# An encoder step on one core: the first norm by tiles, queries ahead of keys, the first values as parts, fp32 averages, and two output tiles on GpSimd

## The reference, cut to what matters

```python
def rms_norm(x, g):
    y = x * lax.rsqrt(jnp.mean(x * x, axis=-1, keepdims=True) + EPS)
    return y * g
for l in range(DEPTH):
    h = rms_norm(xp, ln_mix[l])
    qa, ka, va, fa, qb, kb, vb = split(h @ w_in[l])
    logf = log_sigmoid(fa + b_f)
    c = cumsum(logf)                       # decay of each key, per head
    # 8 forgetting heads of 64, causal, softmax(q k * scale + c_q - c_k) @ v
    # then: sliding-window heads, output projection, memory attention, gated convolution
y = rms_norm(x, ln_final)
```

## Time and profile before

| what | value |
|---|---|
| median of 3 runs | 3360.53 us (3358.93 to 3365.29) |
| the profiled execution's own time | 3357.14 us |
| its span, first to last instruction | 3355.3 us |
| granted TensorE clock, mean | 0.991 |
| busy: TensorE 96%, weight loads 93% | VectorE 56%, POOL 36%, ScalarE 25% |
| moved by DMA | 177.57 MB |

### The profile page before, as it was taken

One profiled execution on the slowest core, in us unless ns is written; L12 is line 12 of the kernel. 1 busy time (PEld: TensorE's weight loads), 2 busy tenths in 40 slices (PEclk: granted clock), 3 DMA queues, 4 the chain that ended last, 5 costly groups with the idle time before them and its releaser, 6 DMA issues.

```text
span 3355.3 us, 50277 instructions
## 1 busy us (share of the span) xinstructions
PE 3219.7 (96%) x20496; PEld 3110.7 (93%) x20496; DVE 1893.9 (56%) x3526; ACT 843.9 (25%) x1950; POOL 1210.8 (36%) x976
## 2 busy tenths in 40 slices
PE   7999998999999999999999999989999999999997
PEld 7888898888999999999988988978889999999996
DVE  6655557676744444444665656576756444444445
ACT  4432324543300000000233333154433000000002
POOL 5213223542433333333442122443425333333331
PEclk9999999999999999999999999999999999999998
DMA  4111222211111111111122111321111111111111
GB/s 161 52 52 45 65 66 69 64 45 31 37 44 46 45 45 46 43 45 47 39 78 59 52 52 46 92 68 51 42 29 42 45 45 45 42 45 47 45 45 65
DMA packets 86021, 177.57 MB, mean 53 GB/s; under 512 B 10544, under 2 KB 13872, under 8 KB 85392
## 3 DMA queue, kind: packets, MB, share of 16 engines
q1 hardware_dynamic: 71968, 132.90, 13.7%
q10 hardware_dynamic: 13824, 41.46, 4.3%
HBM read 150.36 MB, written 16.29 MB: 50 GB/s over the span
## 4 chain that ended last, share of the span: by engine, by line
PE 80%; DVE 10%; ACT 6%; issue 2%; POOL 1%; DMA 0%; ACTq 0%; DVEq 0%; SPq 0%; POOLq 0%
PE PS L614 80%; DVE ACC L1636 2%; ACT PR L1262 2%; DVE HL L1628 1%; DVE PR L1717 1%; DVE XT L1760 1%; ACT PW L1262 1%; DVE PW L1717 1%; ACT PTH L1114 1%; DVE XT L1590 1%; DVE PTL L1562 1%; POOL WL L594 1%; POOL WH L592 1%; DVE DG L1675 0%; ACT G0H L1114 0%
## 5 line engine op out<-in xcount | busy, mean ns | idle before, releaser
L592 POOL TENSOR_TENSOR WH<-RAW,zero 128x512 fp32r<-128x512 f32 x484 | 549.4, 1135 | 2059.1 <-PE PS L614 2044.5
L614 PE MATMUL PS<-HH,WH 128*128 128x384 f32 (+1 forms) x3312 | 861.6, 332 | 26.5 <-DVE HL L1628 17.1
L614 PE MATMUL PS<-HH,WL 128*128 128x384 f32 (+1 forms) x3312 | 848.9, 328 | 0.0
L614 PE MATMUL PS<-HL,WH 128*128 128x384 f32 (+1 forms) x3312 | 848.4, 328 | 0.0
L594 POOL TENSOR_TENSOR WL<-RAW,WH 128x512 fp32r<-128x512 f32 x484 | 666.8, 1378 | 37.9
L614 PEld LDWEIGHTS PS<-HH,WH 128*128 128x128 f32 x3312 | 587.1, 189 | 37.3 <-issue 19.3
L614 PEld LDWEIGHTS PS<-HL,WH 128*128 128x128 f32 x3312 | 590.2, 189 | 0.0
L614 PEld LDWEIGHTS PS<-HH,WL 128*128 128x128 f32 x3312 | 589.7, 188 | 0.0
L1760 DVE TENSOR_TENSOR XT<-PS,XT 128x320 f32<-128x320 f32 x464 | 314.3, 719 | 264.1 <-PE PS L614 264.0
L614 PE MATMUL PS<-G0H,WH 128*128 128x384 f32 (+1 forms) x960 | 274.9, 339 | 25.1 <-DVE XT L1590 16.4
L1114 ACT ACTIVATE PTH<-PS 128x512 fp32r<-128x512 f32 (+4 forms) x320 | 165.5, 520 | 493.7 <-PE PS L614 492.4
(11 more groups left out here) (255 smaller groups left out, 4704.4 us busy)
## 6 DMA issues: line engine op xcount, KB each, us to landing
RAW<-in_slabs SPq DMA_DIRECT2D x484, 256.0 KB, 2.6
XR<-decays ACTq DMA_DIRECT2D x16, 512.0 KB, 5.8
XT<-in_xT SPq DMA_DIRECT2D x8, 544.0 KB, 8.4
out_fk<-T ACTq DMA_DIRECT2D x8, 544.0 KB, 2.7
XR<-decays ACTq DMA_DIRECT2D x16, 272.0 KB, 7.0
out_fv<-T ACTq DMA_DIRECT2D x8, 544.0 KB, 3.3
out_y<-YT ACTq DMA_DIRECT2D x8, 544.0 KB, 3.1
RX<-ST ACTq DMA_DIRECT2D x24, 136.0 KB, 3.1
```

The source lines that it names most:

```text
L592: pool.tensor_tensor(WH[:, s, :], RAW[:, s, :], zero[:, 0:1].to_broadcast([128, HALF]), ALU.add).then_inc(w_hi, 1)
L614: ins = pe.matmul(*a, **k)
```

## The change

- Order of slabs: f, q0, k0, ck0, v0, cv0 in place of f, k0, q0, v0, ck0, cv0. Pair 0's values become three parts in its own attention, as in the other pairs. The 64 own scores of the sample are made after the first of them (`late`), once the keys are split.
- Layer 0 reads tile after tile (`project_first`) and makes the average from four sums of two squares each, by fp32 products between the tiles (`first_stat`).
- All averages are one product in fp32 (`mean` by `ACC`) without a split. The last one adds the last two squares by products of their own (`last_stat`). The average of the memory tokens moves to the beginning of layer 0.
- `inverse_rms` does columns 768 to 1087 first and signals twice; readers of `R` wait for the second signal where they need it (`await_all_rms`).
- The bias transfers have three semaphores, the sample's first.
- At the end `R` is put in PSUM for VectorE and in `ACC` for POOL; ScalarE scales two tiles, POOL multiplies them by `R`, SP sends them; VectorE does six.
- `slab_pair` becomes `slab_halves` in parts, in `down` and in the cached scores: the wait for the second half-slab stands where its first product is.

```diff
-    order = ["f", ("k", 0), ("q", 0), ("v", 0)]
+    order = ["f", ("q", 0), ("k", 0)]
     for p in range(PAIRS):
-        order += [("ck", p), ("v", p), ("cv", p)] if p else [("ck", p), ("cv", p)]
+        order += [("ck", p), ("v", p), ("cv", p)]
...
+            for kt in range(POOL_Y):
+                sp.wait_ge(y_pool, kt + 1)
+                sp.dma_start(o_y[:, kt, :], YT[:, kt, :]).then_inc(out_done, 16)
...
+            pool.wait_ge(r_copied, 1)
+            for kt in range(POOL_Y):
+                pool.wait_ge(y_scaled, kt + 1)
+                pool.tensor_tensor(YT[:, kt, :], YT[:, kt, :], ACC[:], ALU.mult).then_inc(y_pool, 1)
...
+            def slab_halves(pe, key):
+                slots = [slab(pe, key)]
+                slots.append(place.n["slab"] % 4)
+                place.add("slab")
+                return slots, place.at("slab")
...
+            def project_first(pe, key):
+                s = claim(pe)
+                for kt in range(KT):
+                    if kt % 4 == 0:
+                        slot = slab(pe, key)
+                    pe.wait_ge(h_ready, kt + 1)
+                    c = slice((kt % 4) * 128, (kt % 4 + 1) * 128)
+                    products(pe, s, [[(w[:, slot, c], x[:, kt, :]) for w, x in ((WH, HH), (WH, HL), (WL, HH))]], CH,
+                             kt == 0, kt == KT - 1)
...
+                    if kt in (2, 4, 6):
+                        first_stat(pe, kt // 2 - 1)
...
+            def first_stat(pe, pair):
...
+                pe.wait_ge(sq_used, pair + 1)
+                for (a, b), o in zip(CH, STAT):
+                    mm(pe, PS[:, o:o + b - a], mean, FIRST_SQ[2 * pair][:, a:b], start=pair == 0, stop=pair == KT // 2 - 1)
...
                     if m % 4 == 0:
-                        slots = slab_pair(pe, keys[m // 4])
+                        slots, second = slab_halves(pe, keys[m // 4])
...
-                    if m == 0 and late is not None:
+                    if m % 4 == 0:
                         products(pe, s, steps[:1], CH, True, False)
-                        pe.wait_ge(*late)
+                        pe.wait_ge(w_ready, second)
...
                 for kt in range(KT):
+                    if kt == 4 and c == order[0]:
+                        pe.wait_ge(w_ready, second)
...
             def stat(pe):
-                pe.wait_ge(stat_ready, place.at("norm", 1))
+                pe.wait_ge(sq_used, place.at("norm", KT - 1, KT - 1))
...
-                for k, x in enumerate((SH, SL)):
-                    for (a, b), o in zip(CH, STAT):
-                        mm(pe, PS[:, o:o + b - a], mean_r[:], x[:, a:b], start=k == 0, stop=k == 1)
+                for (a, b), o in zip(CH, STAT):
+                    mm(pe, PS[:, o:o + b - a], mean, ACC[:, a:b], start=True, stop=True)
...
+            def last_stat(pe):
...
+                for x, ready in ((ACC, (sq_used, place.at("norm", KT - 3, KT - 1))),
+                                 (SQ[(KT - 3) % SQS], (sq_ready, place.at("norm", KT - 1, KT))),
+                                 (SQ[(KT - 2) % SQS], (sq_ready, place.at("norm", KT, KT)))):
...
+                    if s < 0 and steps[0]["kind"] == "fox_s" and steps[0]["late"]:
+                        pe.wait_ge(attn_ready, place.at("attn", 1))
+                        place.add("attn")
+                        own_scores(pe)
...
-                project_late(pe, ("k", 0))
-                project(pe, ("q", 0), HH, HL, CH)
-                project(pe, ("v", 0), HH, HL, CH)
+                project_late(pe, ("q", 0), stat if l else lambda pe: None)
+                if l == 0:
+                    mem_stat(pe)
+                project(pe, ("k", 0), HH, HL, CH)
...
-            def inverse_rms(act):
+            def inverse_rms(act, out=R):
                 act.wait_ge(stat_done, place.at("norm", 1))
...
+                act.activation(out[:, 768:T], R[:, 768:T], ACT.Exp, scale=-0.5).then_inc(rms_ready, 1)
+                act.activation(out[:, 0:768], R[:, 0:768], ACT.Exp, scale=-0.5).then_inc(rms_ready, 1)
...
+                biases(0, (2,))
                 filled(act)
-                hi(act, [(QH[:], QLS)])
-                biases(0)
...
+                hi(act, [(KH[:], STAGES[0])])
+                biases(0, (0, 1))
+                act.dma_start(o_fk[l * PAIRS], STAGES[0]).then_inc(k0_out, 16)
...
+                fill(dve, QLS, stored=False)
                 dve.wait_ge(ln_done, place.at("layer", 1))
+                dve.tensor_tensor(FL[:], FL[:], FA[:], ALU.subtract).then_inc(lf_ready, 1)
...
-            for kt in range(KT):
-                dve0.scalar_tensor_tensor(YT[:, kt, :], XT[:, kt, :], FC[:, kt:kt + 1], R[:], ALU.mult, ALU.mult)\
+            for kt in range(POOL_Y, KT):
+                dve0.scalar_tensor_tensor(YT[:, kt, :], XT[:, kt, :], FC[:, kt:kt + 1], RP, ALU.mult, ALU.mult)\
                     .then_inc(y_ready, 1)
```

More of the change, by code:

```diff
@@ L201, in encoder_step @@
         mean_r = sb("mean_r", [128, 128], F32R)
+        mean = mean_r[:].bitcast(F32)
         causal_r = sb("causal_r", [128, 128], F32R)
@@ L346, in over_tile @@
                     ins.then_inc(third_free if a == 768 else free[s], 1)
+                if a == 768 and between is not None:
+                    between()
             return ins
@@ L838, in mem_stat @@
             def mem_stat(pe):
-                s = claim(pe)
-                pe.wait_ge(mstat_ready, 1)
-                for k, x in enumerate((MSH, MSL)):
-                    mm(pe, PS[:, s * 1024:s * 1024 + MEM], mean_r[:], x, start=k == 0, stop=k == 1)
-                done(s)
+                pe.wait_ge(msq_used, 1)
+                pe.wait_ge(rms_ready, 2)
+                for c in range(2):
+                    mm(pe, PS[:, (6 + c) * 512 + 384:(7 + c) * 512], mean, MACC[:, c * 128:(c + 1) * 128], start=True, stop=True)
+                signal(mstat_ready, now=True)
             def value_tiles(pe, src, tiles_of, rows_of, filled):
@@ L921, in scores, with own_scores @@
                     signal(w_used)
-                    pe.wait_ge(g_free, place.at("group", 1))
-                    b = (6 + place.n["group"] % 2) * 512
-                    product(b, DEC, QSH[:], QSL[:], KH[:, SEQ:T], KL[:, SEQ:T], tail_mask_r)
-                    signal(g_full, now=True)
-                    place.add("group")
+                    if not st["late"]:
+                        own_scores(pe)
+            def own_scores(pe):
+                pe.wait_ge(g_free, place.at("group", 1))
+                b = (6 + place.n["group"] % 2) * 512
+                out = PS[:, b:b + DEC]
+                for k, (q, key) in enumerate(((QSH, KH), (QSH, KL), (QSL, KH))):
+                    mm(pe, out, q[:], key[:, SEQ:T], start=k == 0, stop=False)
+                mm(pe, out, ident_r[:], tail_mask_r[:], start=False, stop=True)
+                signal(g_full, now=True)
+                place.add("group")
             def transposes(pe, st, s):
@@ L1563, in lo, with fill @@
                 return ins
-            def fill(dve, out, stored=True):
+            def fill(dve, out, stored=True, between=None):
                 if stored:
@@ L1684, in attention @@
                 for s in range(n + 3):
-                    if s and ahead:
+                    early = s > 0 if ahead else s == 0 and steps[0]["late"]
+                    if early:
                         parts_out(s - 1, 2)
@@ L1693, in attention @@
                             place.add("bias")
-                            waits.append((bias_in, place.at("bias", 0, 64)))
+                            waits.append((bias_in[2], place.at("bias", 0, 32)))
+                        if s in (1, 2) and st["kind"] == "fox":
+                            waits.append((bias_in[st["h"]], place.at("bias", 0, 16)))
                         if s >= 3:
@@ L1722, in attention @@
                         place.add("use")
-                    if s == 0 or not ahead:
+                    if not early:
                         parts_out(s - 1, 2)
```

255 lines of the change are left out of this document (134 added, 121 removed).

## The result

The changed kernel took 3333.45 us (median of 4 runs, 3332.84 to 3337.11), the kernel before 3359.73 beside it; the ratio is 0.9924, with a 95% interval of 0.991 to 0.9939. The profiled execution took 3332.84 of its own, with a span of 3330.8. The prediction had 3336, a span of 3330.8 and a range from 3324 to 3350. The sum on the span is met to the tenth, and the median is 2.6 us lower than forecast: the 3.4 us that the prediction put between a profiled execution and the median were 0.6. Most terms of the sum are off, and their errors cancel.

What follows compares the result with a forecast made beforehand. TensorE's idle time and number of products were taken to set the time. Terms -4.0 - 5.7 - 6.0 - 6.2 - 2.6 = -24.5 us on a span of 3355.3 gave 3330.8, 3336 as a median, range 3324 to 3350.

Steps and rivals of the forecast that it cites:

- Averages in the middle: Five norm averages in layers 0 and 1: the 1.79 us wait goes, fp32 products take 1.9; -1.0 us each.
- Layer 0's beginning: Layer 0's first projection and averages: TensorE starts at about 10.4, ends at 33; cached scores of pair 0 start at 57.5.
- Pair 0's start: Pair 0 in both layers: value parts fill TensorE's idle time around the softmax; -5.7 and -6.0 us, together -11.7.
- Bias transfers: Pair 0's bias transfers, issued with less cover before VectorE reads them: priced at nothing, up to 5 us a layer.
- Half-slab waits: TensorE's waits for second half-slabs, moved to their first product: 3.1 us a layer, -6.2 us; new inner waits cost nothing.
- The end: Last average and output: average ends at 3334.5 instead of 3337.4, output stays bound by DMA engines; -2.6 us.
- Cheap fp32: Rival on the averages: fp32 records cost by width as in fp32r, each average 0.9 us less; 3326; 8%.
- The late bias: Rival in pair 0: bias transfers 5 us late in each layer, VectorE waiting for a DMA; 3346; 12%.
- The slow clock at the start: Rival in layer 0: small gaps at every tile keep TensorE's first 18 us at the lower clock; +13, 3349; 7%.
- Waits within the stream: Rival: 120 new waits drain TensorE's queue; 3348 at 0.1 us each, 3372 at 0.3; 7% in all.
- nothing comes of it: Rival: VectorE bounds pair 0 and half-slabs come late, so only the averages and the end stay; 3354; 4%.

Runs made afterwards that it cites:

- both_orders: Changed kernel with VectorE's `QSL` subtraction moved behind the scaling of `C8`, and layer 1's keys' high half taken ahead of the bias transfers on ScalarE; 3330.77 us.
- changed_again: The changed kernel word for word, run again as the yardstick for its group; 3333.09 us.
- split_averages: Changed kernel with the five averages in the middle made from an fp32r split again, six fp32r products each; 3339.54 us.
- one_average_end: Changed kernel with the last average made of one sum again: VectorE adds all eight tiles of squares, TensorE makes one fp32 average; 3336.18 us.
- decays_sooner: Changed kernel with VectorE's subtraction for `QSL` moved behind the scaling of `C8`, so the decays are stored sooner; 3329.18 us.

## Why the prediction was right, and where not

*Averages in the middle.* The wait of 1.79 went, as predicted, and no other wait took its place. The product was mis-sized: I took 1.9 us, scaled from products of 128 columns, and it is 1.6. The Trainium skill, "FP8 and Floating Point Precision", section "TensorE Precision Notes", has four passes for a true fp32 product, an estimated 1.8 us for an average. The trace does not agree: 1.59 us for 1088 columns are 3.5 cycles a column at 2.4 GHz, and the measurement decides. That each product is two records, which I had read as agreement, says nothing of the number of passes. That makes -6.5 for the five. I also took nothing for the clock: in the kernel before it is at 0.50 behind two of the five waits, and there the ledger has 1.1 and 1.3 more.

```profile
898.00:900.00 2.00, 2.00 (x7) 2.00 (x7) 0.00 (x0) 1.97 (x4) 0.00 (x0) 0.50 0.00 0
2393.00:2395.00 2.00, 2.00 (x8) 2.00 (x8) 0.00 (x0) 1.98 (x3) 0.00 (x0) 0.50 0.00 0
```

The last 1.3 of the ledger's -10.2 (predicted: -5.0) are small shifts beside the five places that no run takes apart, and no run shows that the waits caused the two falls.

*Layer 0's beginning.* First product at 10.54 (10.4 predicted), the last average at 32.48 with `R` begun at 34.5 (33), cached scores at 58.58 (57.5). The waits for tiles were 2.1 us, not 1.

*Pair 0's start.* Here the reason failed. "what goes is the idle time around the softmax (...) and it is filled by the values' 12 us" gave the right stretch in layer 0 (26.69 against 26.5), but 2.8 of the gain of 3.8 us are there without the parts; 1.3 of them come from the Exp table that is loaded ahead, 0.6 lie between the places of the transpositions or in the clock, and 0.9 stay open. In layer 1 the stretch was 29.19 in place of 26.5: I had "`C8` at 1710", 2.9 us before the keys end at 1712.9; it came 0.24 before their end, and ScalarE's order put the keys' high half behind the store. I had looked for the price of that in the bias, up to 5 us a layer, and not in what is queued on ScalarE behind its wait for the store. With the decays sooner the stretch is 26.39.

*Bias transfers.* I priced them at nothing, rightly: in both_orders VectorE waits 2.13 us for them and TensorE's stretch does not change.

*Half-slab waits.* They gave -7.2 against -6.2: one wait of 0.7 us a layer is left, where I had expected two of about 1.2 and 0.5. The 120 inner waits cost nothing, as 2483 more of them show.

*The end.* -3.1 against -2.6; both arguments (pieces of the average, an output bound by the DMA engines) are shown by a kernel each.

*The rivals.* Cheap fp32 (0.9 us less for each average) came true by a third: it is 0.3 less. The late bias was half right: there was a loss in layer 1's pair 0, but it came by way of the keys. The slow clock at the start cost 1.8 us (twelve products in 3.77 us, from 10.54 to 14.31, in place of 2.0) where the sum had 2. Waits within the stream and "nothing comes of it" are excluded.

The span came out exactly because errors of -5.2 (averages), -1.0 (half-slabs) and -0.5 (the end) stood against +1.3 (layer 0's beginning), +2.9 (layer 1's pair 0) and +2.5 (the clock). The direction and the range were earned; that the sum met the span was luck.

## What to carry to other kernels

In a chain of waits, open each piece of the stretch that you mean to fill, those without a tile's name above all: a table load of 1.28 us there was as good a target as 12 us of products. Where an engine waits for a store before it may issue the transfers that read it, ask what else stands in its queue, and finish the stored tile first. 2483 more satisfied waits cost TensorE nothing here, so put each wait at the first product that needs it. And where the clock moves medians by more than the term in question, compare the stretch that the edit touches, and look in the records of the clock before you put the rest down to the edit.

## What the runs showed of the hardware that was not expected

The clock does not follow the gap alone. In the stretch of layer 0's pair 0 the changed kernel has waits of 0.98 and 0.66 us and stays at 1.00. In another execution (changed_again) the clock falls behind the first wait, of 0.99 us, and the second is 0.40. Windows of the one and the other:

```profile
84.00:88.00 4.00, 4.00 (x38) 4.00 (x36) 1.96 (x5) 0.60 (x1) 0.94 (x1) 1.00 0.00 0
```

```profile
84.00:88.00 4.00, 3.60 (x18) 3.58 (x17) 2.46 (x7) 0.27 (x1) 0.00 (x0) 0.50 0.00 0
```

That is 2.0 us (a stretch of 28.68 in place of 26.69), and five of the ten profiled executions with value parts in pair 0 fall there. In two of the five, split_averages and one_average_end, the clock then stays at 0.50 for 27.3 and 23.9 us, though TensorE is busy for 8.00 of 8.00 us in windows of that time; these two executions are the slowest runs of their kernels. The gap of 2.5 us in the ledger is alike: in layer 0 it ends at 547.27 in the kernel before, where the clock is 1.00 in the 5 us behind it, and at 540.15 in the changed one, where it is 0.66. Of the kernel before, eleven runs on one chip lie between 3353.59 us at a mean clock of 0.993 and 3372.23 at 0.987: 0.006 of the span is 20 us, and the spread is 18.6, so the clock can be all of it. The changed kernel's six runs on that chip lie within 6.9 us, at 0.994 to 0.996.

At the very start the clock's column is not a measurement. It says 1.00 while the products take twice as long: the products of 320 columns are 0.27 us apart, and the first tile takes 2.86 us (10.54 to 13.40), where the same nine products take 1.60 later on (17.09 to 18.69). The trace of the changed kernel holds no record of the clock ahead of 14.52 us, and the column shows 1.00 where it has none. In each of the fourteen traces the products run at the lower rate up to the first record, which stands at 14.5 to 18.7 us and says 1.00, and at the higher rate behind it. Two products, and a window (columns as in the earlier trace rows):

```profile
12.60 0.47 PE L625 MATMUL PS<-HH,WH 128*128 128x320 f32 x1
12.87 0.47 PE L625 MATMUL PS<-HL,WH 128*128 128x320 f32 x1
```

```profile
10.50:12.50 2.00, 1.96 (x6) 1.99 (x7) 1.40 (x1) 2.00 (x3) 2.00 (x2) 1.00 1.01 409
```

VectorE and POOL are slow at the same time. In layer 1 POOL's subtraction takes 3.16 us in place of its usual 1.29, under VectorE's scan of `C8` (1693.38 to 1696.39) and the first half of `QSL`, which takes 2.14. In decays_sooner, where `QSL` comes elsewhere, the subtraction takes 3.16 again, under two scans, and `QSL` takes 1.45. In layer 0 POOL stands still until 52.88, and `QSL` takes 0.46. No run here takes POOL's work away from the same place, so this is a coincidence in time, seen at these places, and no more. The changed kernel, POOL in layer 1, then VectorE in layer 0:

```profile
1694.33 3.16 POOL L601 TENSOR_TENSOR WL<-RAW,WH 128x512 fp32r<-128x512 f32 x1
```

```profile
52.56 0.46 DVE L1643 TENSOR_TENSOR QSL<-QLS,QSH 64x64 fp32r<-64x64 f32 x2
```
